# Rotary half swaps as SBUF-to-SBUF transfers issued by ScalarE, in place of products with a permutation matrix

## The reference

```
def apply_rope(t, cos, sin):
    half = t.shape[-1] // 2
    t1, t2 = t[..., :half], t[..., half:]
    return concatenate([t1 * c - t2 * s_, t2 * c + t1 * s_], axis=-1)

def swa_sink_branch(q, k, v, sinks, cos, sin):
    qh = apply_rope(q.reshape(b, s, SWA_Q_HEADS, SWA_HEAD_DIM), cos, sin)
    kh = apply_rope(k.reshape(b, s, SWA_KV_HEADS, SWA_HEAD_DIM), cos, sin)
    ...
```

## Time and profile before

| | |
|---|---|
| median of 3 runs | 2321.98 us (2320.55 to 2325.04) |
| the profiled execution | 2324.64 us, its span 2322.8 us |
| TensorE busy | 2253.6 us, 97% of the span |
| VectorE busy | 1024.1 us, 44% |
| ScalarE busy | 812.9 us, 35% |
| GpSimd busy | 117.2 us, 5% |
| granted TensorE clock, mean | 0.99 |

### The profile page before, as it was taken

How to read it: one execution, slowest core, us unless ns; L and a number is a source line. 1 busy time by engine, 2 the same in 40 slices (tenths; PEclk the granted TensorE clock), 3 DMA queues, 4 the chain that set the end, 5 groups by cost and what they waited for, 6 DMA issues and landing times.

```text
span 2322.8 us, 29589 instructions
## 1 busy us (share of the span) xinstructions
PE 2253.6 (97%) x11656; PEld 1881.8 (81%) x11656; DVE 1024.1 (44%) x1416; ACT 812.9 (35%) x1371; POOL 117.2 (5%) x126
## 2 busy tenths in 40 slices
PE   7999999988999999999999999999799999999998
PEld 7888888767887888888888888887678878888887
DVE  4434324683435544432253443248634364443423
ACT  5322215531543432322252322256235335332321
POOL 0000001121000100000000000012110001000000
PEclk9999999999999999999999999999899999999999
DMA  4322322221122332233233232232211223322222
GB/s 159 100 99 91 100 100 91 100 62 49 58 71 83 134 110 100 90 99 100 82 109 99 91 99 99 92 119 74 62 55 50 79 89 130 111 97 99 93 97 82
DMA packets 67416, 215.15 MB, mean 93 GB/s; under 512 B 15216, under 2 KB 15984, under 8 KB 66800
## 3 DMA queue, kind: packets, MB, share of 16 engines
q1 hardware_dynamic: 65584, 201.10, 26.1%
q0 software_dynamic: 1728, 12.58, 1.5%
HBM read 206.84 MB, written 6.82 MB: 92 GB/s over the span
## 4 chain that ended last, share of the span: by engine, by line
PE 90%; DVE 5%; ACT 2%; issue 1%; DMA 1%; DVEq 0%; SPq 0%; ACTq 0%
PE ps L507 20%; PE ps L509 20%; PE ps L508 20%; PE ps L551 8%; PE ps L553 8%; PE ps L552 8%; DVE tmp L1442 1%; DVE wlo L1262 1%; DMA raw<-in_wstream_dram 1%; PE ps L519 1%; PE ps L726 1%; DVE ulo L1302 1%; ACT uhi L959 1%; PE ps L787 1%; DVE tmp L1430 0%
## 5 line engine op out<-in xcount | busy, mean ns | idle before, releaser
L1262 DVE TENSOR_TENSOR wlo<-raw,whi 128x1024 fp32r<-128x1024 f32 (+1 forms) x376 | 466.4, 1241 | 914.3 <-ACT whi L909 904.0
L507 PE MATMUL ps<-uhi,whi 128*128 128x512 f32 (+1 forms) x2208 | 834.8, 378 | 11.2 <-DVE ulo L1302 8.7
L509 PE MATMUL ps<-uhi,wlo 128*128 128x512 f32 (+1 forms) x2208 | 824.2, 373 | 0.0
L508 PE MATMUL ps<-ulo,whi 128*128 128x512 f32 (+1 forms) x2208 | 824.1, 373 | 0.0
L909 ACT ACTIVATE whi<-raw 128x1024 fp32r<-128x1024 f32 (+1 forms) x372 | 389.6, 1048 | 967.8 <-PE ps L509 592.0
L507 PEld LDWEIGHTS ps<-uhi,whi 128*128 128x128 f32 x2208 | 420.2, 190 | 90.0 <-DVE ulo L1302 9.9
L509 PEld LDWEIGHTS ps<-uhi,wlo 128*128 128x128 f32 x2208 | 419.5, 190 | 73.3
L508 PEld LDWEIGHTS ps<-ulo,whi 128*128 128x128 f32 x2208 | 420.2, 190 | 71.5 <-issue 1.0
L551 PE MATMUL ps<-whi,hhi 128*128 128x512 f32 x704 | 274.4, 390 | 0.0
L553 PE MATMUL ps<-whi,hlo 128*128 128x512 f32 x704 | 274.0, 389 | 0.0
L552 PE MATMUL ps<-wlo,hhi 128*128 128x512 f32 x704 | 273.9, 389 | 0.0
(11 more groups left out here) (220 smaller groups left out, 1633.3 us busy)
## 6 DMA issues: line engine op xcount, KB each, us to landing
raw<-in_wstream_dram SPq DMA_DIRECT2D x368, 512.0 KB, 3.5
x_home<-x POOLq DMA_DIRECT2D x2, 2048.0 KB, 7.9
x<-x_home POOLq DMA_DIRECT2D x2, 2048.0 KB, 8.9
gain<-in_gp_dram POOLq DMA_DIRECT2D x6, 512.0 KB, 5.5
x<-in_x_dram SPq DMA_DIRECT2D x4, 512.0 KB, 7.0
raw<-in_wstream_dram SPq DMA_DIRECT2D x8, 256.0 KB, 2.8
out_dram<-x SPq DMA_DIRECT2D x8, 256.0 KB, 2.0
rcs<-in_rope_dram POOLq DMA_DIRECT2D x2, 512.0 KB, 10.6
```

The source lines that it names most:

```text
L507: pe.matmul(o, lh, bhi, start=first, stop=False)
L508: pe.matmul(o, lh, blo, start=False, stop=False)
L509: return pe.matmul(o, ll, bhi, start=False, stop=last)
L1262: dve.tensor_tensor(wlo[:, s, 0:cols], raw[:, s % RAWS, 0:cols], whi[:, s, 0:cols].bitcast(f32), ALU.subtract) \
```

## The change

For each rotated tile the product with the permutation matrix is gone from TensorE, and so are two uses each of PSUM banks 2 and 3 and one of bank 5. Behind `evac 15` ScalarE waits for its own copy, and then issues eight transfers within SBUF: four move the quarters of query tiles 0 and 1 into buffer `swap_a`, four those of tiles 2 and 3 into `swap_b`, each to the partitions of the other half. Each has 32 partitions x 8 x 128 float32, 128 KB. Behind `evac 17` it issues four more, 32 x 8 x 64 (64 KB), for the key. The sign is now in the sine table. VectorE multiplies the swapped copy in place and adds as before. The buffers lie over memory that was free or is freed by then, hence new waits: `evac 17` waits for the fourth rotated tile, `evac 18` for the fifth, and the transfers wait for copies long done. VectorE no longer waits for its own last sum before it goes on.

```diff
+        swap = [at("swap_a", [P, NCH, 2, CH], 148 * kb), at("swap_b", [P, NCH, 2, CH], 94.5 * kb)]
...
-                    elif k == "rope":
-                        i, b = step[1], banks_of(step)[0]
-                        use(L, step, b)
-                        pe.wait_ge(m_read.h, m_read.at(L, 16 if i < 4 else 17))
-                        done(pe.matmul(bank(b), con[:, K_ROT:K_ROT + P], attn_in(i), start=True, stop=True), b)
...
+                            elif i in (17, 18):
+                                act.wait_ge(roped.h, roped.at(L, i - 13))
...
                             act.activation(dst, chunks(bank(b)) if 12 <= i < 16 else bank(b), ACT.Copy).then_inc(m_read.h, 1)
+                            if i in (15, 17):
+                                act.wait_ge(m_read.h, m_read.at(L, i + 1))
+                                if i == 15:
+                                    for n in range(2):
+                                        act.wait_ge(misc_out[4 + n].h, misc_out[4 + n].at(L, USE[("off", n), 4 + n] + 1))
+                                else:
+                                    act.wait_ge(roped.h, roped.at(L, 2))
+                                for n in range(2 if i == 15 else 1):
+                                    for q in range(4):
+                                        p, r = 32 * q, 32 * (q ^ 1)
+                                        if i == 15:
+                                            act.dma_start(swap[n][p:p + 32], sq[r:r + 32, :, 2 * n:2 * n + 2, :]).then_inc(swap_in[n].h, 16)
+                                        else:
+                                            act.dma_start(swap[0][p:p + 32, :, 0, :], chunks(sk[r:r + 32, :])).then_inc(swap_in[2].h, 16)
...
                     elif k == "rope":
-                        i, b = step[1], banks_of(step)[0]
-                        ready(step, b)
+                        i = step[1]
                         dve.wait_ge(rope_in.h, rope_in.at(L, 16))
-                        link(L, dve.tensor_tensor(tmp[:, 2 + i % 2, :], bank(b), rcs[:, 1, :], ALU.mult))
+                        swapped = swap[i // 2 % 2][:, :, i % 2, :]
+                        dve.wait_ge(swap_in[i // 2].h, swap_in[i // 2].at(L, 64))
+                        link(L, dve.tensor_tensor(swapped, swapped, chunks(rcs[:, 1, :]), ALU.mult))
                         dve.wait_ge(rot_cos.h, rot_cos.at(L, i + 1))
                         if i < 4:
-                            dve.tensor_tensor(attn_in(i), chunks(tmp[:, 2 + i % 2, :]), chunks(tmp[:, i % 2, :]), ALU.add).then_inc(roped.h, 1)
+                            dve.tensor_tensor(attn_in(i), swapped, chunks(tmp[:, i % 2, :]), ALU.add).then_inc(roped.h, 1)
...
-                        dve.wait_ge(roped.h, roped.at(L, i + 1))
-                        dve.sem_inc(misc_out[b].h, 1)
```

More of the change, by code:

```diff
@@ L65 @@
 NPAR = C_BA + 64
-K_ID, K_ONE, K_TRI, K_STRICT, K_ROT = (P * i for i in range(5))
-K_S64 = 5 * P
+K_ID, K_ONE, K_TRI, K_STRICT = (P * i for i in range(4))
+K_S64 = 4 * P
 K_I64, K_TRI64, K_M01 = K_S64, K_S64 + 64, K_S64 + 128
@@ L159, in banks_of @@
         return (7, 4) if x == 0 else (6, 7)
-    if k == "rope":
-        return (2 + x % 2,) if x < 4 else (5,)
     if k == "wt":
@@ L388, in trunk @@
         roped = sem("roped", 5)
+        swap_in = [sem(f"swap_in{i}", 64) for i in range(3)]
         eq_done = sem("eq_done", 1)
@@ L1537, in do @@
                     elif k == "rope":
-                        i, b = step[1], banks_of(step)[0]
-                        ready(step, b)
+                        i = step[1]
                         dve.wait_ge(rope_in.h, rope_in.at(L, 16))
-                        link(L, dve.tensor_tensor(tmp[:, 2 + i % 2, :], bank(b), rcs[:, 1, :], ALU.mult))
+                        swapped = swap[i // 2 % 2][:, :, i % 2, :]
+                        dve.wait_ge(swap_in[i // 2].h, swap_in[i // 2].at(L, 64))
+                        link(L, dve.tensor_tensor(swapped, swapped, chunks(rcs[:, 1, :]), ALU.mult))
                         dve.wait_ge(rot_cos.h, rot_cos.at(L, i + 1))
                         if i < 4:
-                            dve.tensor_tensor(attn_in(i), chunks(tmp[:, 2 + i % 2, :]), chunks(tmp[:, i % 2, :]), ALU.add).then_inc(roped.h, 1)
+                            dve.tensor_tensor(attn_in(i), swapped, chunks(tmp[:, i % 2, :]), ALU.add).then_inc(roped.h, 1)
                         else:
-                            dve.tensor_tensor(skz[0:CH, 0, :], tmp[0:CH, 2, :], tmp[0:CH, 0, :], ALU.add)
-                            dve.tensor_tensor(skz[CH:P, 1, :], tmp[CH:P, 2, :], tmp[CH:P, 0, :], ALU.add).then_inc(roped.h, 1)
-                        dve.wait_ge(roped.h, roped.at(L, i + 1))
-                        dve.sem_inc(misc_out[b].h, 1)
+                            dve.tensor_tensor(chunks(skz[0:CH, 0, :]), swapped[0:CH], chunks(tmp[0:CH, 0, :]), ALU.add)
+                            dve.tensor_tensor(chunks(skz[CH:P, 1, :]), swapped[CH:P], chunks(tmp[CH:P, 0, :]), ALU.add).then_inc(roped.h, 1)
                     elif k == "sc":
@@ L1806, in constants @@
     half = CH // 2
-    for m in range(P):
-        d = m % CH
-        c[m + half if d < half else m - half, K_ROT + m] = -1.0 if d < half else 1.0
     r, q = (i % CH)[:, None], np.arange(CH)[None, :]
@@ L1821, in constants @@
     ang = np.arange(SEQ, dtype=np.float32)[None, :] * inv.astype(np.float32)[:, None]
-    rope = np.stack([np.tile(np.cos(ang), (4, 1)), np.tile(np.sin(ang), (4, 1))], 1)
+    rope = np.stack([np.tile(np.cos(ang), (4, 1)), np.concatenate([-np.sin(ang), np.sin(ang)] * 2)], 1)
     return c, np.ascontiguousarray(rope.astype(np.float32))
```

## The result

| | before | after |
|---|---|---|
| median | 2321.51 us (2320.55 to 2325.04) | 2340.55 us (2339.58 to 2341.55) |
| profiled execution, its span | 2324.64, 2322.8 | 2341.2, 2339.4 |
| mean granted clock | 0.99 | 0.983 |

The ratio is 1.0079, with a 95% interval of 1.0067 to 1.0092. The change made the kernel 19.0 us slower. The forecast was 4.4 us slower, and 2340.55 lies outside the range of 2320.5 to 2332. The direction was right, the size was not.

A forecast was written before the change was run, and what follows sets the result against it. TensorE, busy 97%, was taken as the bound, paced by ScalarE's queue to `lst 2` and VectorE's to L1484. Per layer 4.0 + 0.9 - 0.8 - 1.9 = +2.2, twice +4.4: 2326.4 us, range 2320.5 to 2332.

The forecast's parts named there:

- The eight issues: ScalarE's queue ahead of the Tanh and `lst 2`: eight query transfer issues take 3.8 us, delaying TensorE by +4.0 per layer.
- A slower restart: TensorE from `lst 2` to `lst 3`: the longer wait of 5.7 us brings the low clock behind it, +0.9 per layer.
- the four query products: TensorE ahead of its wait for bank 5: not on the path, so removing them only lengthens the wait for VectorE.
- VectorE's chain: VectorE from `lst 3` to the first L1484: fewer waits (-0.56, -0.84), GpSimd contention (+0.6), together -0.8 per layer.
- its bound of -0.2: VectorE's term if each of GpSimd's two cosine products also blocks the sine products; the time would go to 2327.6.
- The key: TensorE between the last transpose and chunk 20: removing the key's product and its wait for bank 5 gives -1.9 per layer.
- the 0.3 us of cover: ScalarE behind `evac 17`: four key issues take 1.9 us, ending 0.3 us before ScalarE's next work, so they cost nothing.
- VectorE waits for a transfer: Sign at VectorE's use of the swapped tiles that the forecast is wrong; `swap_a` was expected with 7 us of cover.
- Dear issues: Rival: ScalarE's issues overlapping SyncE's second group take double, first term 7.8, +12.0 in all, 2334.0 us; chance 0.12.
- Cheap issues: Rival: ScalarE's issues cost 0.05 us each, the restart term vanishes, -2.1 per layer, 2317.8 us; chance 0.09.
- Late query transfers: Rival: `swap_a` lands 13 us behind its last issue, VectorE waits 2.4 us, +4.8 in all, 2331.2 us; chance 0.09.
- The range: Whole kernel: 2320.5 to 2332 us for 8 in 10, cutting most of the rivals' far ends; forecast's own 2322.5 to 2330.

The follow-up runs named there:

- four larger issues: The change with four query transfers of 256 KB on ScalarE in place of eight of 128 KB: 2330.0 us, 1.0035.
- The test with spare products: Matrix products that nobody reads, added in TensorE's three long waits: kernel before 2312.98 us (0.9964), the change 2318.44 us (0.9988).
- the kernel without any transfer: The change with the exchange of halves left out, VectorE multiplying the unswapped tile: 2320.19 us, 0.999.
- the issues alone: Kernel before plus the change's twelve ScalarE transfers at the same places, their data used by nothing: 2339.83 us, 1.0078.
- the key alone: Kernel before with only the key's product replaced by four ScalarE transfers, query products kept: 2318.73 us, 0.9986.
- the filled change: The change with 20, 28 and 24 unread TensorE products ahead of `lst 0`, `lst 2` and the second value transpose: 2318.44 us, 0.9988.
- SyncE's filled kernel with its transfers first: The change with SyncE issuing all transfers, the queries' ahead of its `blk` group, plus 20, 6, 15 unread products in TensorE's waits: 2311.27 us, 0.9961.
- the filled kernel of before: Kernel before with 20, 6 and 15 unread TensorE products ahead of `lst 0`, `lst 2` and the second value transpose: 2312.98 us, 0.9964.

## Why the prediction was wrong

**The eight issues: the right place, the wrong size.** The step "I take 3.8 us, the row of the same instruction with as many runs in each" failed. They took 5.45 us, 0.68 each, and the term was +5.58 and not +4.0. Equal numbers of runs do not make equal issues: SyncE's groups in the earlier trace rows move 16 KB each, these 128 KB, and with 256 KB an issue took 0.80 us. Among these the price grows with the bytes, but slowly, and it falls on whoever issues. This is 1.6 us a layer, and with the clock held it is what the sum missed: +5.8 - 1.0 - 1.9 = +2.9 a layer, against +2.2 foretold.

**The clock: the term that failed.** "A slower restart", +0.9, took the low clock as ending with `lst 3`. Up to there it was 1.65 and 1.78 us, since the wait was 7.3 us and not 5.7; with four larger issues the wait was 5.1 us and the row +0.7 and +0.8, near what was foretold for 5.7. But there was more: TensorE was granted the lower level in stretches where it had not been, the last some 50 us behind the second long wait (0.83 in the mean over 580 to 590). The shift table has +3.3 us in the first layer and +4.2 in the second outside that row, where the forecast had nothing. The windows of before showed the pattern, 0.91 and 0.74 where TensorE waits twice, 1.00 from 540 on; I had looked at one window of 5 us and at the rows right behind the waits. The test with spare products gives the size: with the clock mostly held, the change costs 5.5 us and not 19, so 13.5 us came with the low clock where the forecast had 1.8.

Where those 13.5 us arise is only in part shown. The row of `lst 3` follows the wait ahead of `lst 2` in every kernel without spare products: 3.8 to 5.3 us from `lst 2` to `lst 3` behind 1.7 us, 6.05 behind 5.1, 6.6 to 7.0 behind 7.3. The other stretches don't: the one in the layer's tail also stands in the kernel without any transfer (3.1 us) and not in the one with the issues alone. The forecast had another term at nothing as well. It took the four query products as worthless since TensorE waits behind them. They are not on the path, but they fill that wait: with them it is 4.0 us, without them 6.3 to 6.7, and the kernels without them have the lower granted clock. Where ScalarE issues no query transfers the median execution has 0.989 or 0.990 without them (three kernels) and 0.992 with them (before, and the key alone); where it issues eight, 0.983 against 0.988. The kernels of such a pair differ in more than the query products, so this is not shown to be the cause.

**VectorE's chain: right.** -0.8 was foretold, -0.84 and -0.89 measured. The rows show both sides of it, no gaps, and a sum and a sine product that are long beside GpSimd's products (1.65 and 1.74 us, where 0.69 is usual). These two cost 2.0 us, 0.7 more than the 1.34 of before, where +0.6 was taken:

```profile
524.73 1.65 DVE L1556 TENSOR_TENSOR sq<-swap_a,tmp 128x512 f32<-128x512 f32 x1
526.31 1.21 DVE L1273 TENSOR_TENSOR wlo<-raw,whi 128x1024 fp32r<-128x1024 f32 x1
527.44 1.74 DVE L1553 TENSOR_TENSOR swap_b<-swap_b,rcs 128x512 f32<-128x512 f32 x1
...
524.17 1.66 POOL L1765 TENSOR_TENSOR tmp<-sq,rcs 128x512 f32<-128x512 f32 x1 [6.86 <-DVE sq L1556]
526.46 2.18 POOL L1765 TENSOR_TENSOR tmp<-sq,rcs 128x512 f32<-128x512 f32 x1 [0.63 <-DVE sq L1556]
```

The Trainium skill, "SBUF — State Buffer", section "Who interferes with whom", says that a VectorE instruction with two SBUF inputs contends with a GpSimd instruction that reads SBUF. The trace after agrees: the sine product at 527.44, now with two SBUF inputs, took 1.74 us beside GpSimd. That the term would go to its bound of -0.2 by this rule did not come true, since only that one of the four sine products was held up; the one at 524.01 had begun when GpSimd's came, and it was GpSimd's that took 1.66 us.

**The key: right.** -1.9 was foretold, -1.93 and -1.91 measured, and between -1.89 and -1.93 in every kernel that moved it. Its four issues took 2.6 us and not 1.9, more than the 0.3 us of cover, and Pm came right behind them at 553.32; TensorE did not wait for it, as the text had said. The sign "VectorE waits for a transfer" did show, by 1.12 us for the key's, and cost TensorE nothing:

```profile
556.17 0.69 DVE L1553 TENSOR_TENSOR swap_a<-swap_a,rcs 128x512 f32<-128x512 f32 x1 [1.12 <-DMA swap_a<-sk]
```

**The rivals.** Dear issues was wrong as a mechanism, although the issues were dearer: they cost the same without a second issuer. Sharing does exist, but on the other side and where the overlap is longer. SyncE's `blk` group takes 3.76 us in the change and 5.22 in the filled change, where it runs beside most of ScalarE's eight issues; there those of `swap_a` land 5.1 us behind their issue, while the issues themselves go only from 0.68 to 0.70 us. The two kernels:

```profile
505.17 3.76 SPq L490 DMA_DIRECT2D blk<-sol_home  x8
```

```profile
503.57 5.22 SPq L490 DMA_DIRECT2D blk<-sol_home  x8
```

Cheap issues is refuted by 0.68 us each. Late query transfers did not happen in the change (2.8 and 2.4 us), but did where SyncE issued them behind `blk`. That the query products were off the path was right, VectorE's chain and not they set the second transpose; what they did to the clock was overlooked.

**The range** took in the bounds of single terms, but no term of the clock that comes on top of the forecast's own, and the clock was the largest term of the result.

## What to carry to other kernels

A transfer has a price on the queue of the engine that issues it, mostly 0.5 to 0.8 us here and 0.33 for a weight load, so twelve issues must stand where their engine has nothing due that another waits for; the same twelve issues alone cost 17.5 us with eight of them ahead of a due square, and the change with them on SyncE was 3.5 us faster than before. Where a change lengthens a wait of TensorE, read the granted clock in windows over the whole stretch behind it and not only right behind the wait; a kernel that keeps TensorE busy there tells the clock's share from the wait's. Products with a permutation matrix that lie in front of a wait for another engine cost nothing and shorten that wait, and only the one that chunk 20 stood behind was worth moving: the fastest kernel here moves the key alone.

## What the runs showed of the hardware that was not expected

- An issue of a transfer within SBUF of 32 partitions mostly took 0.61 to 0.70 us for 64 KB, 0.64 to 0.72 us for 128 KB and 0.78 to 0.80 us for 256 KB (ScalarE alone), on ScalarE as on SyncE for the others; single groups of four reached 0.95 us each (64 KB, SyncE) and 0.80 (128 KB, ScalarE).
- 41 spare products in each layer, which compute nothing, made the kernel before 9 us faster (2312.98 against 2322.3), by a granted clock of 1.00 where it was 0.74 to 0.91. In the kernel before this is 4.7 us a layer that TensorE loses by waiting, beside the waits themselves.
- The kernels in which TensorE had fewer products to do were granted a lower clock. With no exchange and no issues the mean is 0.988 to 0.991, against 0.990 to 0.994 before. In SyncE's filled kernel with its transfers first TensorE waited 3.66 us and was granted 0.83 in 520 to 540, where the filled kernel of before waited 0.54 and had 1.00.
- Kernels with the same work and the same wait of 5.3 us took 8.57 to 10.13 us from `lst 0` to `lst 1`, by how long the low clock lasted. A low-clock row of one trace is not a change's effect until other kernels show it.
